# Sending products of layer B's output projection into its last attention segment

## What is computed

```python
q, k, v, g = jnp.split(u @ w_in, 4, axis=-1)          # 16 heads of 64
...
p = jax.nn.softmax(jnp.concatenate([s, s_ctx], axis=-1), axis=-1)
o = jnp.einsum('bhnqrj,brnjhd->bnqhd', p_lat, v_reg) + jnp.einsum('bhnqc,bchd->bnqhd', p_ctx, vc)
...
y = (o * jax.nn.silu(g)) @ w_out                      # the output projection
...
h = layer_norm(DEEPNORM_ALPHA * h + gate[:, None, :] * y, ln_g[i], ln_b[i])
```

## Time and profile before

| | us |
|---|---|
| median of three runs | 3215.78 |
| profiled execution, its own time | 3218.72 |
| its span on the core | 3216.7 |
| TensorE busy in the span | 3098.5 (96%) |
| granted TensorE clock, mean | 0.988 of full |

### The profile page before, as it was taken

How to read it: one execution, slowest core, us unless ns; L and a number is a source line. 1 busy time by engine, 2 the same in 40 slices (tenths; PEclk the granted TensorE clock), 3 DMA queues, 4 the chain that set the end, 5 groups by cost and what they waited for, 6 DMA issues and landing times.

```text
span 3216.7 us, 47790 instructions
## 1 busy us (share of the span) xinstructions
PE 3098.5 (96%) x18114; PEld 2574.5 (80%) x18114; DVE 2004.9 (62%) x3838; ACT 1300.8 (40%) x2340; POOL 762.1 (24%) x324
## 2 busy tenths in 40 slices
PE   9999999999999989999899999999999999999987
PEld 6888888777777767877798989988677777877765
DVE  5676677555565656975855555555855555655556
ACT  5534443444444440022444434440344444544422
POOL 3223332222222213443211121114112121111121
PEclk9999999999999999999999999999999999999999
DMA  3111111111111137621200010044201111101142
GB/s 118 46 40 47 46 60 46 60 53 60 53 53 53 59 152 290 218 94 52 92 31 30 31 44 31 30 165 155 104 27 52 45 52 45 45 21 51 42 180 85
DMA packets 64828, 237.79 MB, mean 74 GB/s; under 512 B 7008, under 2 KB 10080, under 8 KB 63600
## 3 DMA queue, kind: packets, MB, share of 16 engines
q1 hardware_dynamic: 32832, 120.11, 10.8%
q10 hardware_dynamic: 31792, 114.91, 9.6%
HBM read 185.11 MB, written 49.87 MB: 73 GB/s over the span
## 4 chain that ended last, share of the span: by engine, by line
PE 81%; DVE 9%; ACT 4%; issue 2%; DVEq 2%; DMA 1%; ACTq 1%; SPq 0%
PE ps L1318 22%; PE ps L189 13%; PE ps L360 9%; PE ps L2244 7%; PE ps L1382 5%; PE ps L1348 5%; PE ps L1364 4%; PE ps L891 3%; PE ps L482 3%; PE ps L868 2%; PE ps L133 1%; PE ps L852 1%; DVE fox_l L1469 1%; DVE wa_l L941 1%; PE ps L853 1%
## 5 line engine op out<-in xcount | busy, mean ns | idle before, releaser
L210 POOL TENSOR_TENSOR w_hi<-raw,small 128x1024 fp32r<-128x1024 f32 x160 | 337.1, 2107 | 2376.5 <-PE ps L1318 1081.6
L212 POOL TENSOR_TENSOR w_lo<-raw,w_hi 128x1024 fp32r<-128x1024 f32 x160 | 424.9, 2656 | 22.8
L1318 PE MATMUL ps<-nb_u_hi,w_hi 128*128 128x512 f32 (+1 forms) x640 | 249.6, 390 | 6.4 <-DVE nb_q_lo L2491 4.5
L1318 PE MATMUL ps<-nb_u_hi,w_lo 128*128 128x512 f32 (+1 forms) x640 | 246.3, 385 | 0.0
L1318 PE MATMUL ps<-nb_u_lo,w_hi 128*128 128x512 f32 (+1 forms) x640 | 246.2, 385 | 0.0
L1480 DVE TENSOR_TENSOR nb_pt_lo<-ps,nb_pt_hi 128x512 fp32r<-128x512 f32 x208 | 143.8, 691 | 136.5 <-ACT nb_pt_hi L1407 136.1
L360 PE MATMUL ps<-u_hi,w_hi 128*128 128x512 f32 x528 | 213.1, 404 | 5.9 <-ACT silu_h L539 2.6
L360 PE MATMUL ps<-u_hi,w_lo 128*128 128x512 f32 x528 | 208.7, 395 | 0.0
L1318 PE MATMUL ps<-u_hi,w_hi 128*128 128x512 f32 x512 | 208.4, 407 | 0.0
L1318 PE MATMUL ps<-u_hi,w_lo 128*128 128x512 f32 x512 | 208.2, 407 | 0.0
L360 PE MATMUL ps<-u_lo,w_hi 128*128 128x512 f32 x528 | 208.2, 394 | 0.0
(11 more groups left out here) (359 smaller groups left out, 8017.4 us busy)
## 6 DMA issues: line engine op xcount, KB each, us to landing
raw<-in_w_stream SPq DMA_DIRECT2D x160, 512.0 KB, 3.4
h_sb<-in_w_ada ACTq DMA_DIRECT2D x16, 1024.0 KB, 5.5
nf_b<-nf_rows ACTq DMA_DIRECT2D x16, 512.0 KB, 4.5
nb_bias<-in_rel_bias ACTq DMA_DIRECT2D x16, 448.0 KB, 4.1
y_parts<-wa_y_hi ACTq DMA_DIRECT2D x8, 640.0 KB, 3.0
y_parts<-wa_y_lo ACTq DMA_DIRECT2D x8, 640.0 KB, 4.2
la_out_yh<-y_parts SPq DMA_DIRECT2D x8, 640.0 KB, 10.1
la_out_yl<-y_parts SPq DMA_DIRECT2D x8, 640.0 KB, 10.8
```

The costliest lines, as they stand in the source:

```text
L210: pool.tensor_tensor(w_hi[:, s, :], raw[:, s, :], zero, ALU.add)
L212: pool.tensor_tensor(w_lo[:, s, :], raw[:, s, :], w_hi[:, s, :].bitcast(F32), ALU.subtract).then_inc(w_ready, 1)
L1318: mm = pe.matmul(ps[:, b:b + ch["n"]], w(slot, k), u[:, k, ch["c0"]:ch["c0"] + ch["n"]], start=k == 0 and p == 0, stop=k == KT - 1 and p == 2)
```

## The change

`Flow.plan` gets a number `beside_last`, 4 for layer B, and writes an "R" step into the last turn: four matmuls of a generator behind each of the last segment's seven T steps, and six ahead of the last V step, 34 in all. The generator, `Layer.first_pair`, makes the 96 matmuls of the output projection's tiles 0 and 1: k tiles 0 to 6 of tile 0 (two chunks), the same of tile 1, and then k tile 7 of both. What is left of it after the turn runs at once behind it. The loop of `Layer.pe` begins at pair 1 for layer B (`Fori(self.l, ...)`; for layer A, `self.l` is 0 and nothing changes).

```diff
@@ plan, in the last turn
                             fill_to((at["fill"] + goal) // 2)
+                            if final_turn and seg == len(groups) - 1 and beside_last:
+                                steps.append(("R", beside_last))
                             if i == 0:
@@
+                    if final_turn and beside_last:
+                        steps.append(("R", 6))
                     steps.append(("V", waiting))
@@ Flow.pe
+                    elif step[0] == "R":
+                        for _ in range(step[1]):
+                            next(after)
@@ Layer.pe
-                with pe.Fori(0, KT // 2) as i:
+                with pe.Fori(self.l, KT // 2) as i:
@@ Layer
+            def first_pair(self, pe, mixer):
+                def products(m, c, tiles):
+                    t, n = self.chunks[c]
+                    out = ps[:, 3 * m * CH + t:3 * m * CH + t + n]
+                    for k in tiles:
+                        for p, (w, y) in enumerate(((whi, self.yh), (whi, self.yl), (wlo, self.yh))):
+                            mm = pe.matmul(out, w(m, k), y[:, k, t:t + n], start=k == 0 and p == 0,
+                                           stop=k == KT - 1 and p == 2)
+                            if k == KT - 1 and p == 2:
+                                mm.then_inc(w_used if c else self.chunk, 1)
+                            yield mm
+
+                for m, banks in ((0, (0, 1)), (1, (3, 4))):
+                    pe.wait_ge(w_ready, self.n_out + m + 1)
+                    for s, v in [w for b in banks for w in mixer.free(b)]:
+                        pe.wait_ge(s, v)
+                    if m == 0:
+                        pe.wait_ge(self.y_first, 32 * (KT - 1) * (self.l + 1))
+                    for c in range(2):
+                        yield from products(m, c, range(KT - 1))
+                for m in range(2):
+                    for c in range(2):
+                        if m == 0:
+                            pe.wait_ge(*((self.y_last, 32 * (self.l + 1)) if c else
+                                         (self.y_early, 32 * len(mixer.early))))
+                        yield from products(m, c, [KT - 1])
@@ nb_pe
+            after = layer_b.first_pair(pe, nb)
             for steps in nb.turns:
-                nb.pe(pe, steps, flow, before_scores)
+                nb.pe(pe, steps, flow, before_scores, after)
+            for _ in after:
+                pass
```

More of the change, by code:

```diff
@@ L1112, in pieces_until, with plan @@
                 return last
-            def plan(self, before, turns, final, tables, last_fill, side_by_side=False, ahead_by=0):
+            def plan(self, before, turns, final, tables, last_fill, side_by_side=False, ahead_by=0, beside_last=0):
                 self.chunks = []
@@ L1325, in projected, with pe @@
                 return ps[:, ch["bank"] * CH:ch["bank"] * CH + ch["n"]]
-            def pe(self, pe, steps, flow, before):
+            def pe(self, pe, steps, flow, before, after=None):
                 for step in steps:
@@ L2420, in build_program @@
                 {"Q": "dve", "K": "dve", "V": "act", "G": "act"}, 2,
-                sum(len(nb.seg_groups(seg)) for seg in range(2)), True, 1)
+                sum(len(nb.seg_groups(seg)) for seg in range(2)), True, 1, 4)
         def nb_pe(pe):
```

## The result

The changed kernel takes **3226.49 us** (median of 9 runs, 3222.22 to 3233.63) against 3217.49 us (9 runs of before on the same chip): ratio **1.002**, 95% interval 1.0011 to 1.0028. It is slower by 9.0 us.

What follows compares the result with a forecast made beforehand. TensorE, busy 96%, and the queue behind y were taken to bound the kernel. Tile 2's start +7.5 and clock +2.2 gave +9.7 us, 3228.4 profiled; the median, 2.94 lower, was 3225.4 us, range 3218.5 to 3229.5.

Steps and rivals of the forecast that it cites:

- Step 1: At the last segment's first product, TensorE stands 7.3 us for the last of 14 copies of y.
- Step 2: In the last segment, stall and packed products make the fifth T step 9.1 us later, plus 2.2 us of clock.
- X: Delay of the last segment and of the y copies and queue behind it: 9.1 + 2.2 = 11.3 us.
- The loss of clock: TensorE running half fast after the segment's stall: 2.2 us, bounds 0 and 3.9.
- Step 3: Tiles 0 and 1 get shorter behind the segment, ending at 3110.2; TensorE alone would be 1.9 us early for tile 2.
- step 4: Tile 2 waits for its weights, queued behind y, and their split: start +7.5 us, plus 2.2 us of clock.
- slack: Before the change, the split of tile 2's weights ended 3.8 us ahead of need, hiding X in part.
- the same company comes again: GpSimd's split of tile 2's weights again runs beside VectorE's first tile; without it about 1.7 us shorter.
- y is there in time: Rival: no wait at the first product; tile 2 gains 2.1 us, which the clock gives back; 3213.7 to 3216, 6%.
- Tile 2's weights don't wait for the segment: Rival: weights are early, TensorE bounds and tile 2 starts 1.9 us sooner; 3213.9, 5%.
- the change's full gain: Rival: even without segment delay, only the 3.8 us until tile 2's split ends are gained; 3212.0, 1%.

Runs made afterwards that it cites:

- e1: Changed kernel, but the segment's 34 products read resident keys instead of y, with the wait for `y_first` behind them: 3214.02 us, ratio 0.9996.
- e2: Changed kernel with one product behind each T step of the last segment in place of four: 3224.14 us, ratio 1.0018.
- e4: Changed kernel with 52, 20 and 22 filler matmuls ahead of the waits for `y_first`, the late copies and tile 2: 3229.21 us, ratio 1.0038.
- e7: Changed kernel with the weights of tiles 2 and 3 queued between the first and the early copies of y: 3228.34 us, ratio 1.0024.
- e9: e7 with ScalarE's three 512 KB loads held back until the late copies of y have landed: 3223.90 us, ratio 1.0018.
- e3: Changed kernel with no product inside the segment, all 96 running behind it in the new order: 3214.85 us, ratio 0.9995.
- e6: Changed kernel with products only behind the last two T steps and ahead of the last V step, 14 in all: 3217.51 us, ratio 0.9990.
- e5: Changed kernel with shorter fillers, 29, 9 and 11 matmuls, ahead of the same waits as in e4: 3227.15 us, ratio 1.0018.
- e8: e6 with the weights of tiles 2 and 3 queued between the first and the early copies of y: 3216.79 us, ratio 0.9991.

## Why the prediction was right, point by point

Forecast: 3225.4 us, range 3218.5 to 3229.5, slower at 0.74. Measured: 3226.49, slower. The profiled execution was put at 3228.4 and took 3229.05. The closeness of the numbers is in part luck: the forecast counted from 3215.78 (three runs of before), where nine runs give 3217.49.

*Step 1, the wait.* Right in cause and size. Forecast 7.3 us from the T step to the product; measured 3076.75 - 3069.34 - 0.38 = 7.0, idle 6.78, ended by the DMA that was named. e1 (wait gone, work kept) and e2 (work mostly gone, wait kept) show that it is the wait. Of the traffic, 0.03 of the engines' share is left from 3076.0 and the landing comes at 3076.61, about 0.5 us behind its end. The 2 us of the Trainium skill (DMA: Bandwidth & Descriptors, section on the anatomy of one DMA), whose figures there are for DMAs issued by GpSimd, do not show on this DMA of SyncE, nor in the earlier trace rows.

*Step 2, the packed segment and X.* From the first product to the fifth T step I had 9.4 us, clock included; measured 9.03. X was 11.3; the fifth T step moved by 16.44 - 5.86 = 10.6, and the move of L1428 (12.25 us later than in the earlier trace rows, less 1.67) by 10.6 too, so that nothing between them gave or took. The loss of clock was put at 2.2 us here and measured 1.8 by e4, and 2.8 and 2.7 in the executions of e7 and e9.

*Step 3, tiles 0 and 1.* The order of the products came as told: 42 of them ahead of VectorE's last step. The early copies, put ahead of their need, were 1.09 us late. **The sentence that failed** is "up to 9 us of lateness on their part is hidden by step 4": GpSimd's split waits for the slot that tile 0 frees, so only the time until the weights land was there to hide in. The late copies landed 7.3 us after their issue, tile 0's last products started only at 3112.99, and it is these that released GpSimd. The row that would have told stood in the trace of before, from the same window as the loads of the row of factors; I had not read it:

```profile
lb_out_yl<-y_parts SPq DMA_DIRECT2D x1, 128.0 KB, 7.5
```

Before, these copies landed at 3092.08 + 7.5 = 3099.6, and TensorE came to them 24 products behind 3094.87, at about 3100.4. After, TensorE came to them at 3110.3 and they landed at 3112.99. Counted from T0 the copies came 11.7 us later than before (the segment's 10.6, and 1.4 from the stalled issue), and TensorE only 8.3: in both kernels 45 products lie between VectorE's last step and this place, but before the first 21 of them ran mostly at half clock (7.1 us for 4.8), and after they all ran at full. The forecast's own numbers with this row give 3092.08 + 7.5 + 11.3 = 3110.9 for the landing, 2.8 us behind the need. The sum hardly noticed, since the landing of the weights, on which it was built, came only 0.6 us ahead of tile 0's end. I was right about the time at this place because two waits end together; e7 shows that removing the one I had named would have brought nothing.

*Step 4, tile 2.* Forecast +7.5 us for its start, measured 50.8 - 44.4 = +6.4. GpSimd began 10.9 us later (45.39 against 34.49 after T0), not 11.3, and split in 5.17 us from start to end (3114.73 to 3119.90), not 6.10 (3102.16 to 3108.26); TensorE followed 0.24 us behind. So 10.9 - 0.9 + 0.2 - 3.8 of slack = 6.4. The forecast that "the same company comes again" was half right: the low part took 3.14 us beside VectorE again, but the high part 1.89 and not 2.77, since VectorE's scaling of the residual had ended before it. The Trainium skill (SBUF — State Buffer, section on who interferes with whom) lets one of the two hold the port for a whole instruction. By that rule the trace agrees: in e9 it is VectorE whose step takes 2.55 us in place of 1.28, beside GpSimd's low part, which keeps to 2.34. Idle time ahead of tile 2 came in three pieces (1.09, 2.53, 2.94), not as one of 9.4, and the clock fell all the same: it cost 2.2 us by e4, as forecast.

*The sum.* +9.7 forecast in the profiled execution; from T0 to the end +8.7, from 6.4 for tile 2's start and 68.45 - 66.1 = 2.3 for its clock. The medians say +9.0, which makes the start of tile 2 the mis-sized term, by 1.1 us (no more than one execution repeats to). In the profiled execution the 1.67 us by which it was late at T0 made up for that.

*The rivals.* "y is there in time" ended on its first condition. Its worked-out outcome, a gain of about 2 us at tile 2 that the clock gives back, is what e3 did (1.9 us earlier at tile 2, end 0.7 later). e1 had no such gain at tile 2 (44.3), and its time too was that of before. "Tile 2's weights don't wait for the segment" fell with e7. Of "the change's full gain" I wrote that it is at most what the slack gives, 3.8 us until the split ends; e6 starts tile 2 4.5 us earlier, a little more, its split being shorter as well (5.6 us, 3099.78 to 3105.40), and ends 2.5 us earlier.

Left open: why the clock falls close to T0 in some executions (e1, e2, e3, e5, e7) and not in others (before, e4, e6, e8) with the same work ahead of it, and whether a cover of exactly the right length would bring e6 the other 2.0 us.

## What to carry to other kernels

Work moved into an engine's idle time brings its own waits, and on an engine that executes in order they are paid by all that stands behind: look up when the data of the first moved instruction lands, and put it behind that place (with 14 products behind that place e6 ends 2.5 us earlier, with 34 from the first step on the change ends 8.7 later). Then follow the gain to what is released next, and for each of several waits that end there take its own landing from the trace, not only the one that the chain names. An idle time ahead of a long run of products can also cost clock, here about 2 us where it fell, which is as much as such a gain is worth.

## What the runs showed of the hardware

- Two copies of 128 KB from DRAM took 5.7 to 9.3 us to land, in before and in nine kernels, beside three loads of 512 KB issued by ScalarE within about 2 us of them, and 2.6 us without them (e9). The order in one queue does not protect a small copy from another queue's large ones.
- The issue of one of the eight small copies held SyncE's queue for 1.1 to 2.2 us in after, e1, e2, e6, e7, e8 and e9, in different places of the row, where the others took 0.3 to 0.5 us.
- A fall of TensorE's clock to 1.2 GHz cost 1.5 to 2.8 us each time: 1.8 in the segment of after and 2.8 in that of e7; behind tile 2's wait, as the 288 products less 66.2, 1.5 in e2, 2.6 in e3 and 2.7 in e7. The same 2.49 us of idle time ahead of VectorE's last step brought it down in e4, e5, e7 and e9 and not in after and e1. In e5 it fell at 3068, while 58 matmuls ran back to back from 3067.83, with 1.16 us of idle time just ahead of T0; in e3 it fell 0.4 us behind T0 without any of them.
- A 128-column float32 product of constants stands as two matmuls in the trace and takes 0.227 us, as long as one of the 512-column products here.
